# Attention probabilities turned in 32x32 blocks by VectorE, and their product with the values as four 32-row products side by side

## The chip, the cores and the metric

The kernel is one program on one core of a Trainium2 chip. The time is the device time of an execution in microseconds (us). All arithmetic is float32. TensorE (PE) multiplies a stationary operand (up to 128 rows by 128 columns, loaded by a weight load, PEld) with a moving one of up to 512 columns and writes to PSUM, which has eight banks of 512 float32 in each of 128 partitions. VectorE (DVE), ScalarE (ACT) and GpSimd (POOL) work elementwise; SyncE (SP) issues the DMAs.

## The reference, cut to what matters

The program is one encoder layer on two sequences, 1024 and 256 tokens, width 1024, with a recurrent branch, an attention branch, a merge and a feed-forward part. The change touches the attention branch only:

```python
# 8 query heads of 128, 2 key/value heads, head g of a group of 4 shares one key/value head
q = _apply_rope(_rmsnorm(q, q_norm), cos, sin)
k = _apply_rope(_rmsnorm(k, k_norm), cos, sin)
s = jnp.einsum('bqhgd,bkhd->bhgqk', qi, k).astype(jnp.float32) * scale   # scale = 128 ** -0.5
p = jax.nn.softmax(s, axis=-1).astype(v.dtype)
o = jnp.einsum('bhgqk,bkhd->bqhgd', p, v)
```

Each sequence attends within itself, without a mask.

## The kernel before

The layer is a row of stages (encoder_layer, L2028): attention_stage, then scaled_stage, gate_stage, state_stage, merge_stage and tail_stage, each in a Stage whose end is a barrier of all engines. Tokens of both sequences lie side by side, T = 1280 columns: 1024 of the first, 256 of the second.

attention_stage has two parts. The first projects ten heads (two for keys, eight for queries), normalises them and turns them by the position tables; the results lie in qk, head dimension on partitions. Then value_rows (L260) computes the values of ten blocks of 128 tokens and ACT copies them to vt, tokens on partitions. This part is not changed but for where its buffers lie.

The second part works on tiles of 128 queries. For a tile of the first sequence the keys are 1024, for one of the second 256; there are 64 tiles of the first kind and 16 of the second. The steps of a tile t, with c = t % 2 naming the buffer:

- scores(t), PE, L273: one or two products of 512 columns into PSUM banks 2c and 2c+1, queries on partitions, keys along the columns.
- maxima(t), DVE, L412: the maximum of each query over its keys, and that times the negative scale.
- exponents(t), ACT, L354: the exponential of all scores from PSUM to p[c], with the sums of the rows (an instruction of its own that reads the accumulator).
- normalise(t), DVE, L421: the reciprocal of the sum, and p times it.
- transposes(t), PE, L284: p turned in 128x128 blocks, through the identity, into banks 4 and 5.
- transposed(t), one half on ACT (L363) and one on DVE (L430): PSUM to pT, keys on partitions, queries along the columns.
- values(g, ks), PE, L293: for a group g of four tiles (512 queries of one head), or two for the second sequence, eight (two) products of 128 keys each, accumulated in bank 6 + g % 2, which gives the output with the head dimension on partitions.
- output(g), DVE, L439, and the send of it to HBM by SP, L221.

The order is written out by hand: PE does transposes(t), scores(t+2) and a quarter (half) of the value products of the group before, in turn. DVE does transposed(t), normalise(t+1), maxima(t+2) and, after a group's last tile, output(g-1). ACT does transposed(t) and exponents(t+2). Every engine works through its list in order, so an instruction that waits holds up all behind it. Semaphores (s_ready, exp_done, p_done, t_ready, o_ready and so on) carry the order between engines.

Other stages have products that use only part of the 128 rows of the array: in low_piece (L613 on) two of 64 rows, on partitions 0 to 63 and 64 to 127, for banks 6 and 7; in scores of state_stage (L1204 on) pairs of 64 rows and 192 columns for two banks; at L1272 and L1292 products of 32 rows, 32 stationary columns and 32 moving columns, at four different places of the array; at L636 products of 64 rows with 32 stationary columns. A float32 product is two MATMUL instructions (two passes) in the trace, a transpose is one.

Of the kernel before, what the change touches and what calls it, by code (L numbers as in the profile page):

```python
# [131 lines left out]
def attention_stage(nc, hbm, xT, cst, glob, w, ahead):  # L132

    with Stage(nc, "at") as st:
        NH = QH + KVH
        HEADS = (*range(QH, NH), *range(QH))
        cos, sin = st.sb("cos", 128, T), st.sb("sin", 128, T)
        qk = st.sb("qk", 128, NH, T)
        vt = st.sb("vt", 128, T // 128, KVH * HD)
        sq, rt, zr = st.sb("sq", 128, T), st.sb("rt", 128, T), st.sb("zr", 128, T)  # L140
        zq = [st.sb(f"zq{i}", 128, T) for i in range(2)]
# [11 lines left out]
        s_ready, mx_done, nm_done, exp_done, ri_done, p_done, t_ready, t_dve, t_act, o_ready, o_done = st.sems(  # L153
            "s_ready mx_done nm_done exp_done ri_done p_done t_ready t_dve t_act o_ready o_done")
        o_sent = st.sems("o_sent0 o_sent1")
        ones, ident = cst[:, C_ONES:C_ONES + 128], cst[:, C_ID:C_ID + 128]

        GROUPS = [(h, 512 * i, 0, SEQ_S, 4) for h in range(QH) for i in range(2)] + [(h, SEQ_S, SEQ_S, SEQ_P, 2) for h in range(QH)]
        TILES = [(g, i) for g, group in enumerate(GROUPS) for i in range(group[4])]
        FIRST = [sum(x[4] for x in GROUPS[:g]) for g in range(len(GROUPS))]  # L160
        NT = len(TILES)

# [3 lines left out]
        def keys_of(t):  # L166
            return GROUPS[TILES[t][0]][3]

# [4 lines left out]
        def columns(g):  # L173

            return 128 * GROUPS[g][4]

        def halves(t):

            return keys_of(t) // 256

        def values_after(t):

            g, i = TILES[t]
            if g == 0:
                return ()
            kt = GROUPS[g - 1][3] // 128
            n = GROUPS[g][4]
            return range(kt * i // n, kt * (i + 1) // n)
# [4 lines left out]
        def _(sp):  # L193
# [24 lines left out]
            sp.wait_ge(v_ready, T // 128)  # L218
            for c in range(2):
                sp.dma_start(w[:, c, :], hbm["w_in"][B_LOW + c]).then_inc(ahead[c], 16)  # L220
            for g in range(len(GROUPS)):  # L221
                h, t0, _, _, n = GROUPS[g]
                sp.wait_ge(o_done, g + 1)
                sp.dma_start(hbm["o_att"][:, h, t0:t0 + 128 * n], ot[g % 2][:, 0:128 * n]).then_inc(o_sent[g % 2], 16)
            for i in range(2):
                sp.wait_ge(o_sent[i], 16 * len(GROUPS[i::2]))

        @block.tensor
        def _(pe):
# [43 lines left out]
            def scores(t):  # L273
                g, i = TILES[t]
                h, t0, k0, nk, _ = GROUPS[g]
                if t >= 2:
                    pe.wait_ge(exp_done, t - 1)
                for b in range(0, nk, 512):
                    n = min(512, nk)
                    last = pe.matmul(ps[:, 2 * (t % 2) + b // 512, 0:n], qk[:, h, t0 + 128 * i:t0 + 128 * i + 128],  # L280
                                     qk[:, QH + h // (QH // KVH), k0 + b:k0 + b + n], start=True, stop=True)
                last.then_inc(s_ready, 1)

            def transposes(t):  # L284
                pe.wait_ge(p_done, t + 1)
                after(pe, t_dve, t)
                after(pe, t_act, t)
                n = halves(t)
                for k in range(2 * n):
                    last = pe.transpose(ps[:, 4 + k // n, 128 * (k % n):128 * (k % n) + 128], p[t % 2][:, 128 * k:128 * k + 128], ident)  # L290
                last.then_inc(t_ready, 1)

            def values(g, ks):  # L293
                h, _, k0, nk, _ = GROUPS[g]
                kv, n = h // (QH // KVH), columns(g)
                end = FIRST[g] + GROUPS[g][4]
                for k in ks:
                    if k == 0:
                        pe.wait_ge(t_dve, end)
                        pe.wait_ge(t_act, end)  # L300
                        if g >= 2:
                            pe.wait_ge(o_done, g - 1)
                    last = pe.matmul(ps[:, 6 + g % 2, 0:n], vt[:, k0 // 128 + k, HD * kv:HD * kv + HD], pT[g % 2][:, k, 0:n],  # L303
                                     start=(k == 0), stop=(k == nk // 128 - 1))
                    if k == nk // 128 - 1:
                        last.then_inc(o_ready, 1)
# [14 lines left out]
            for t in range(NT):  # L321
                transposes(t)
                if t + 2 < NT:
                    scores(t + 2)
                if TILES[t][0]:
                    values(TILES[t][0] - 1, values_after(t))
            values(len(GROUPS) - 1, range(GROUPS[-1][3] // 128))

        @block.scalar
        def _(act):  # L330
# [32 lines left out]
            def transposed(t):  # L363
                g, i = TILES[t]
                n = halves(t)
                act.wait_ge(t_ready, t + 1)
                if g >= 2 and i == 0:
                    act.wait_ge(o_ready, g - 1)
# [1792 lines left out]
```

## Time and profile before

| | us |
|---|---|
| median of three runs | 3450.26 |
| lowest, highest | 3448.57, 3451.94 |
| the profiled execution | 3442.2 |
| its span | 3440.3 |
| attention scores to last output, in it | 310.1 |

The span runs from the first to the last instruction of the profiled execution. In the trace, at_, ra_, rc_ ahead of a tensor's name is the stage (attention, scaled, state), and tensors from L280 on are those of the second part of attention_stage. A matmul's form names rows and columns of the stationary operand, then partitions and columns of the result. Matmul durations include the way through the array, so one lasts longer than the distance to the next; a run of them is read from start to start. "Idle before" is time in which the engine did nothing ahead of that group, with who ended it.

### The profile page before, as it was taken

How to read it: one execution, taken by the hardware profiler on the slowest of the kernel's cores; microseconds unless marked ns; L12 is line 12 of the kernel's file. 1: busy time of each engine (PE TensorE's matmuls, PEld its weight loads, DVE VectorE, ACT ScalarE, POOL GpSimd, SP SyncE). 2: the span in 40 equal slices, each digit the busy share in tenths (PEclk: the TensorE clock that was granted, in tenths of full speed). 3: DMA queues.
4: the chain of work that ended last, by engine and by line, in shares of the span. 5: the costliest groups of instructions: out<-in, count | busy, mean ns of one | idle time of the engine just before them, and what ended most of it. 6: DMA issues, size and time to landing. Idle time of an engine off the chain costs nothing. (4 is left out here: it accounts for less than half of the span.)

```text
span 3440.3 us, 57213 instructions
## 1 busy us (share of the span) xinstructions
PE 3266.6 (95%) x24648; PEld 2068.7 (60%) x24648; DVE 1830.0 (53%) x3086; ACT 986.6 (29%) x1570; POOL 2.5 (0%) x13
## 2 busy tenths in 40 slices
PE   9999998999999899978888999998999999999997
PEld 4565554555544455567777654566666666666665
DVE  1437773667766479145555432156554545645545
ACT  2334442334333223333333453001321121131121
POOL 0000000000000000000000000000000000000000
PEclk9999999999999999999999999999999999999998
DMA  3210001334543524255443223211121211222211
GB/s 134 69 42 13 16 16 41 118 118 134 177 137 111 185 71 162 103 187 176 146 149 117 85 86 131 105 37 61 46 71 61 82 60 61 74 75 80 78 62 61
DMA packets 200297, 321.76 MB, mean 94 GB/s; under 512 B 50800, under 2 KB 156272, under 8 KB 194928
## 3 DMA queue, kind: packets, MB, share of 16 engines
q1 hardware_dynamic: 200048, 318.12, 27.0%
q8 instruction: 196, 3.21, 0.4%
q14 instruction: 53, 0.43, 0.0%
HBM read 216.50 MB, written 95.03 MB: 91 GB/s over the span
## 5 line engine op out<-in xcount | busy, mean ns | idle before, releaser
L608 PE MATMUL ra_ps<-xT,ring 128*128 128x512 f32 (+1 forms) x1152 | 431.9, 528 | 0.0
L1730 PE MATMUL tl_ps<-merged,pool 128*128 128x320 f32 x1440 | 407.9, 436 | 6.4 <-PEq L108 3.9
L1730 PEld LDWEIGHTS tl_ps<-merged,pool 128*128 128x128 f32 x1440 | 274.9, 191 | 123.8 <-issue 11.9
L608 PEld LDWEIGHTS ra_ps<-xT,ring 128*128 128x128 f32 x1152 | 215.1, 190 | 200.4 <-issue 190.7
L1923 DVE TENSOR_TENSOR oR<-tl_ps,oR 128x320 f32<-128x320 f32 x416 | 202.2, 490 | 151.5 <-PE tl_ps L1730 149.4
L1046 PE MATMUL rg_ps<-xT,ring 128*128 128x512 f32 (+1 forms) x720 | 267.1, 526 | 11.9 <-PEq L108 11.9
L1730 PE MATMUL tl_ps<-tl_Th,pool 128*128 128x320 f32 x720 | 205.2, 436 | 6.1 <-issue 6.1
L1046 PEld LDWEIGHTS rg_ps<-xT,ring 128*128 128x128 f32 x720 | 135.1, 192 | 123.7 <-issue 118.2
L1811 ACT ACTIVATE ring<-tl_ps 128x320 f32<-128x320 f32 x96 | 42.0, 437 | 528.1 <-PE tl_ps L1730 528.1
L1730 PE MATMUL tl_ps<-xT,pool 128*128 128x320 f32 x640 | 182.7, 432 | 0.0
L1929 DVE TENSOR_TENSOR merged<-tl_ps,ring 128x320 f32<-128x320 f32 x96 | 47.2, 492 | 253.1 <-PE tl_ps L1730 135.0
L1730 PEld LDWEIGHTS tl_ps<-tl_Th,pool 128*128 128x128 f32 x720 | 138.2, 192 | 64.5 <-issue 8.3
L1730 PE MATMUL tl_ps<-merged,tl_sums 128*128 128x320 f32 x544 | 163.7, 440 | 12.8 <-DVE oR L1923 7.9
L1216 PE MATMUL rc_ps<-pool 64*128 64x192 f32 x1280 | 151.3, 367 | 12.1 <-POOL pool L1358 6.9
L254 PE MATMUL at_ps<-xT,ring 128*128 128x512 f32 (+1 forms) x432 | 159.1, 521 | 0.0
L1730 PEld LDWEIGHTS tl_ps<-xT,pool 128*128 128x128 f32 x640 | 121.6, 190 | 50.7
L1508 PE MATMUL mg_ps<-xT,ring 128*128 128x512 f32 (+1 forms) x384 | 143.4, 527 | 1.9 <-PEq L108 1.9
L1508 PE MATMUL mg_ps<-oR,ring 128*128 128x512 f32 (+1 forms) x384 | 139.4, 526 | 2.9 <-DVE oR L1561 2.9
L1730 PEld LDWEIGHTS tl_ps<-merged,tl_sums 128*128 128x128 f32 x544 | 103.4, 193 | 62.4 <-issue 23.0
L280 PE MATMUL at_ps<-at_qk 128*128 128x512 f32 (+1 forms) x288 | 130.0, 570 | 0.5 <-ACT at_vt L350 0.5
L360 ACT ACTIVATE at_p<-at_ps,at_nm 128x1024 f32<-128x1024 f32 (+1 forms) x80 | 79.0, 987 | 177.2 <-DVE at_nm L419 177.2
L303 PE MATMUL at_ps<-at_pT,at_vt 128*128 128x512 f32 (+1 forms) x288 | 129.4, 569 | 0.0
(241 smaller groups left out, 4747.9 us busy)
## 6 DMA issues: line engine op xcount, KB each, us to landing
pool<-ub SPq DMA_DIRECT2D x80, 640.0 KB, 5.3
ub<-ra_ub SPq DMA_DIRECT2D x32, 1280.0 KB, 5.4
pool<-in_w_ff SPq DMA_DIRECT2D x32, 1024.0 KB, 4.7
pool<-in_w_ff SPq DMA_DIRECT2D x64, 512.0 KB, 3.2
ring<-in_w_in SPq DMA_DIRECT2D x39, 512.0 KB, 3.4
xT<-in_xT SPq DMA_DIRECT2D x16, 640.0 KB, 8.1
ub<-ra_v SPq DMA_DIRECT2D x16, 640.0 KB, 6.5
mg_gate<-gates SPq DMA_DIRECT2D x16, 640.0 KB, 3.9
```

What stands on the lines that cost most here:

```text
L254: last = pe.matmul(ps[:, z_bank(i) + j, 0:n], w[:, i % 3, 128 * k:128 * k + 128], xT[:, k, t0:t0 + n], start=(k == 0), stop=(k == KT - 1))
L280: last = pe.matmul(ps[:, 2 * (t % 2) + b // 512, 0:n], qk[:, h, t0 + 128 * i:t0 + 128 * i + 128], qk[:, QH + h // (QH // KVH), k0 + b:k0 + ...
L303: last = pe.matmul(ps[:, 6 + g % 2, 0:n], vt[:, k0 // 128 + k, HD * kv:HD * kv + HD], pT[g % 2][:, k, 0:n], start=(k == 0), stop=(k == nk ...
L360: act.activation(p[c][:, 0:n], scores_of(t), ACT.Exp, bias=nm[:, c:c + 1], scale=ATT_SCALE, accum_out=rs[:, c:c + 1]).then_inc(exp_done, 1)
L608: last = pe.matmul(ps[:, bank + j, 0:n], w[c][:, 128 * i:128 * i + 128], xT[:, i, t0:t0 + n], start=(i == 0), stop=(i == KT - 1))
L1046: last = pe.matmul(ps[:, 3 * (b % 2) + j, 0:n], w[b % 3][:, 128 * i:128 * i + 128], xT[:, i, t0:t0 + n], start=(i == 0), stop=(i == KT - 1))
L1216: last = pe.matmul(ps[:, 4 + 2 * (q % 2) + h, 192 * j:192 * j + 192], x[rows, 2 * q + j, CH:3 * CH], x[rows, 2 * q + j, 3 * CH:6 * CH], st ...
L1508: last = pe.matmul(ps[:, 3 * (i % 2) + j, 0:n], w[i % 2][:, 128 * k:128 * k + 128], src[:, k, t0:t0 + n], start=(k == 0), stop=(k == KT - 1))
L1730: last = pe.matmul(bank(n, b), lhs(k), rhs(k), start=(fresh and k == 0), stop=(k == d - 1), skip_group_check=True)
L1811: act.activation(cp[n % 2][:, c, :], bank(n, b), ACT.Copy).then_inc(done, 1)
L1923: dve.tensor_tensor(y, bank(n, b), y, ALU.add).then_inc(done, 1)
L1929: dve.tensor_tensor(hidden(n, i, j), bank(n, b), cp[n % 2][:, c, :], ALU.add).then_inc(done, 1)
```

## The change

The 128x128 turns on PE and the copies of them out of PSUM are gone. Instead DVE turns each 32x32 block of p within its 32 partitions (turn), so that partition 32i + k of pT holds key 32j + k for the queries 32i to 32i + 31 of each tile. Quarter i of the partitions thus has its own queries and the keys of every block j. The product with the values (values) is, for each block of 32 keys, four products of 32 rows: quarter i of pT, 256 columns (32 queries of each of 8 tiles), with the 32 values of the block, into bank 4 + i. For this the values of a block must lie on each of the four quarters: they are written to HBM (vrow), and read back four times in rows of 128 numbers (spread) into v4, for the first key/value head ahead of the first group, for the second piece by piece as the last head of the first is done, for the second sequence likewise.

The scaling by the reciprocal goes from DVE to ACT (normalise), from SBUF to SBUF. A group is now one head's eight tiles (and for the second sequence two groups of eight tiles, four heads each): ten groups in place of 24. The value products of a group come in seven parts beside the next group's tiles 1 to 7. Its output, four banks of 256 columns, is copied by DVE (two banks) and ACT (two), and the next group's first products wait for these copies. The buffers of the projection part lie inside the two halves of pT, which are twice as large.

```diff
 with Stage(nc, "at") as st:
     NH = QH + KVH
     HEADS = (*range(QH, NH), *range(QH))
-    cos, sin = st.sb("cos", 128, T), st.sb("sin", 128, T)
     qk = st.sb("qk", 128, NH, T)
-    vt = st.sb("vt", 128, T // 128, KVH * HD)
...
     p = [st.sb(f"p{i}", 128, SEQ_S) for i in range(2)]
-    pT = [st.sb(f"pT{i}", 128, KT, 512) for i in range(2)]
-    ot = [st.sb(f"ot{i}", 128, 512) for i in range(2)]
+    turned = st.sb("turned", 128, 2 * 8 * SEQ_S)
+    v4 = st.sb("v4", 128, 32, HD)
+    ot = st.sb("ot", 128, SEQ_S)
+    cos, sin, sq, rt, zr, zq0, zq1 = (turned[:, T * i:T * i + T] for i in range(7))
+    zq = [zq0, zq1]
+    vt = turned[:, 7 * T:7 * T + 2 * T].rearrange("p (t c) -> p t c", c=KVH * HD)
+    pT = [turned[:, 8 * SEQ_S * c:8 * SEQ_S * c + 8 * SEQ_S].rearrange("p (j t q) -> p j t q", t=8, q=32) for c in range(2)]
...
+    s_ready, mx_done, nm_done, exp_done, ri_done, p_done, turn_done = st.sems(
+        "s_ready mx_done nm_done exp_done ri_done p_done turn_done")
+    v_stored, v4_ready, part_done, o_dve, o_act, o_sent = st.sems(
+        "v_stored v4_ready part_done o_dve o_act o_sent")
+    ones = cst[:, C_ONES:C_ONES + 128]
+    NG = QH + KVH
+    TILES = [(h, 128 * i, 0, SEQ_S) for h in range(QH) for i in range(8)]
+    TILES += [(h, SEQ_S + 128 * i, SEQ_S, SEQ_P) for h in range(QH) for i in range(2)]
     NT = len(TILES)
+    PARTS = 7
     def keys_of(t):
-        return GROUPS[TILES[t][0]][3]
+        return TILES[t][3]
     def scores_of(t):
         c = t % 2
         return ps[:, 2 * c:2 * c + 2, :].rearrange("p b n -> p (b n)")[:, 0:keys_of(t)]
-    def columns(g):
...
+    def blocks(g):
+        return 32 if g < QH else 8
+    def part(g, i):
+        n = blocks(g)
+        return range(n * i // PARTS, n * (i + 1) // PARTS)
+    def values_of(g, i, j):
+        at = j if g < QH else 8 * (g - QH) + j
+        return v4[32 * i:32 * i + 32, at, :]
+    def quarter(g, i):
+        return ot[:, :].rearrange("p (t i q) -> p i t q", i=4, q=32)[:, i], ps[:, 4 + i, 0:256].rearrange("p (t q) -> p t q", q=32)
     block = st.block()
...
-        sp.wait_ge(v_ready, T // 128)
+        def spread(dst, tokens, kv):
+            n = dst.stop - dst.start
+            for i in range(4):
+                sp.dma_start(v4[32 * i:32 * i + 32, dst, :],
+                             hbm["vrow"][tokens:tokens + 32 * n, HD * kv:HD * kv + HD].rearrange("(j k) d -> k j d", k=32)).then_inc(v4_ready, 16)
+        sp.wait_ge(v_done, T // 128)
         for c in range(2):
             sp.dma_start(w[:, c, :], hbm["w_in"][B_LOW + c]).then_inc(ahead[c], 16)
-        for g in range(len(GROUPS)):
...
+        sp.dma_start(hbm["vrow"].rearrange("(t p) c -> p t c", p=128), vt).then_inc(v_stored, 16)
+        sp.wait_ge(v_stored, 16)
+        spread(slice(0, 32), 0, 0)
+        for g in range(NG):
+            for i in range(PARTS):
+                if g in (QH // KVH - 1, QH - 1):
+                    js = part(g, i)
+                    if g == QH // KVH - 1:
+                        sp.wait_ge(part_done, PARTS * g + i + 1)
+                        spread(slice(js.start, js.stop), 32 * js.start, 1)
+                    elif i == 3:
+                        sp.wait_ge(part_done, PARTS * g + i + 1)
+                        for kv in range(KVH):
+                            spread(slice(8 * kv, 8 * kv + 8), SEQ_S, kv)
+            sp.wait_ge(o_dve, 2 * g + 2)
+            sp.wait_ge(o_act, 2 * g + 2)
+            if g < QH:
+                sp.dma_start(hbm["o_att"][:, g, 0:SEQ_S], ot[:, :]).then_inc(o_sent, 16)
+            else:
+                h = QH // KVH * (g - QH)
+                sp.dma_start(hbm["o_att"][:, h:h + 4, SEQ_S:T], ot[:, :].rearrange("p (h n) -> p h n", h=4)).then_inc(o_sent, 16)
+        sp.wait_ge(o_sent, 16 * NG)
     @block.tensor
     def _(pe):
...
             last.then_inc(v_ready, 1)
         def scores(t):
-            g, i = TILES[t]
-            h, t0, k0, nk, _ = GROUPS[g]
+            h, t0, k0, nk = TILES[t]
...
                 n = min(512, nk)
-                last = pe.matmul(ps[:, 2 * (t % 2) + b // 512, 0:n], qk[:, h, t0 + 128 * i:t0 + 128 * i + 128],
+                last = pe.matmul(ps[:, 2 * (t % 2) + b // 512, 0:n], qk[:, h, t0:t0 + 128],
                                  qk[:, QH + h // (QH // KVH), k0 + b:k0 + b + n], start=True, stop=True)
             last.then_inc(s_ready, 1)
-        def transposes(t):
...
+        def values(g, js):
+            for j in js:
+                if j == 0:
+                    pe.wait_ge(turn_done, 8 * g + 8)
+                    pe.wait_ge(v4_ready, 64 * (1 if g < QH // KVH else 1 + PARTS if g < QH else 3 + PARTS))
+                for i in range(4):
+                    if j == 0 and g:
+                        pe.wait_ge((o_dve, o_act)[i // 2], 2 * g - 1 + i % 2)
+                    last = pe.matmul(ps[:, 4 + i, 0:256], values_of(g, i, j), pT[g % 2][32 * i:32 * i + 32, j].rearrange("p t q -> p (t q)"),
+                                     start=(j == 0), stop=(j == blocks(g) - 1))
+            last.then_inc(part_done, 1)
         for i in range(NH):
             head(i)
...
         scores(0)
         scores(1)
         for t in range(NT):
-            transposes(t)
             if t + 2 < NT:
                 scores(t + 2)
-            if TILES[t][0]:
...
+            if t >= 8 and t % 8:
+                values(t // 8 - 1, part(t // 8 - 1, t % 8 - 1))
+        for i in range(PARTS):
+            values(NG - 1, part(NG - 1, i))
     @block.scalar
     def _(act):
...
             c, n = t % 2, keys_of(t)
             act.wait_ge(nm_done, t + 1)
             if t >= 2:
-                act.wait_ge(t_ready, t - 1)
-                act.wait_ge(ri_done, t - 1)
+                act.wait_ge(turn_done, t - 1)
             act.activation(p[c][:, 0:n], scores_of(t), ACT.Exp, bias=nm[:, c:c + 1], scale=ATT_SCALE,
                            accum_out=rs[:, c:c + 1]).then_inc(exp_done, 1)
-        def transposed(t):
...
+        def normalise(t):
+            c, n = t % 2, keys_of(t)
+            act.wait_ge(ri_done, t + 1)
+            act.activation(p[c][:, 0:n], p[c][:, 0:n], ACT.Copy, scale=ri[:, c:c + 1]).then_inc(p_done, 1)
+        def output(g):
+            act.wait_ge(part_done, PARTS * g + PARTS)
+            after(act, o_sent, 16 * g)
+            for i in range(2, 4):
+                dst, src = quarter(g, i)
+                act.activation(dst, src, ACT.Copy).then_inc(o_act, 1)
         exponents(0)
-        exponents(1)
         for t in range(NT):
-            transposed(t)
...
+            normalise(t)
+            if t + 1 < NT:
+                exponents(t + 1)
+            if t >= 16 and t % 8 == 0:
+                output(t // 8 - 2)
+        for g in range(NG - 2, NG):
+            output(g)
     @block.vector
     def _(dve):
...
             dve.wait_ge(s_ready, t + 1)
             dve.reduce_max(mx[:, c:c + 1], scores_of(t), AX.X).then_inc(mx_done, 1)
             dve.wait_ge(mx_done, t + 1)
-            if t >= 2:
-                dve.wait_ge(exp_done, t - 1)
             dve.tensor_scalar(nm[:, c:c + 1], mx[:, c:c + 1], -ATT_SCALE, None, ALU.mult).then_inc(nm_done, 1)
-        def normalise(t):
-            c, n = t % 2, keys_of(t)
+        def reciprocals(t):
+            c = t % 2
             dve.wait_ge(exp_done, t + 1)
-            if t >= 2:
-                dve.wait_ge(p_done, t - 1)
             dve.reciprocal(ri[:, c:c + 1], rs[:, c:c + 1]).then_inc(ri_done, 1)
-            dve.wait_ge(ri_done, t + 1)
...
+        def turn(t):
+            g, i, n = t // 8, t % 8, keys_of(t)
+            dve.wait_ge(p_done, t + 1)
+            if t == 8:
+                dve.wait_ge(v_stored, 16)
             if g >= 2 and i == 0:
-                dve.wait_ge(o_ready, g - 1)
...
+                dve.wait_ge(part_done, PARTS * (g - 1))
+            dve.transpose(pT[g % 2][:, 0:n // 32, i, :], p[t % 2][:, 0:n].rearrange("p (j k) -> p j k", k=32)).then_inc(turn_done, 1)
         def output(g):
-            n = columns(g)
...
+            dve.wait_ge(part_done, PARTS * g + PARTS)
+            after(dve, o_sent, 16 * g)
+            for i in range(2):
+                dst, src = quarter(g, i)
+                dve.tensor_copy(dst, src).then_inc(o_dve, 1)
         maxima(0)
+        reciprocals(0)
         maxima(1)
-        normalise(0)
         for t in range(NT):
-            g, i = TILES[t]
-            transposed(t)
+            turn(t)
             if t + 1 < NT:
-                normalise(t + 1)
+                reciprocals(t + 1)
             if t + 2 < NT:
                 maxima(t + 2)
-            if g and i == GROUPS[g][4] - 1:
...
+            if t >= 16 and t % 8 == 0:
+                output(t // 8 - 2)
+        for g in range(NG - 2, NG):
+            output(g)
...
 def encoder_layer(nc, hbm):
-for name, shape in (("o_att", [128, KT, T]), ("gates", [2 * KT, 128, T]), ("gd", [128, T]), ("bon", [PAIRS, 128, T]),
+for name, shape in (("o_att", [128, KT, T]), ("vrow", [T, KVH * HD]), ("gates", [2 * KT, 128, T]), ("gd", [128, T]), ("bon", [PAIRS, 128, T]),
```

## Rows read from the trace of the kernel before

**Rows 1.** The page: busy time of each engine, share of the span, instructions.

```profile
PE 3266.6 (95%) x24648; PEld 2068.7 (60%) x24648; DVE 1830.0 (53%) x3086; ACT 986.6 (29%) x1570; POOL 2.5 (0%) x13
```

**Rows 2.** Windows: stretch, length, busy time of engines (instructions), granted clock, DMA share, GB/s.

```profile
239.86:549.95 310.09, 297.48 (x1120) 163.49 (x1120) 218.41 (x424) 123.36 (x240) 0.00 (x0) 1.00 0.06 21
261.80:520.00 258.20, 258.20 (x961) 140.98 (x960) 182.22 (x319) 104.13 (x185) 0.00 (x0) 1.00 0.04 16
1500.00:1925.00 425.00, 374.06 (x11780) 324.15 (x11778) 233.76 (x517) 152.43 (x335) 0.00 (x0) 0.96 0.45 144
```

**Rows 3.** Timeline of PE: start us, length us, engine, line, operation, count.

```profile
402.69 1.88 PE L280 MATMUL at_ps<-at_qk 128*128 128x512 f32 x4
404.41 1.88 PE L303 MATMUL at_ps<-at_pT,at_vt 128*128 128x512 f32 x4
406.12 1.04 PE L290 MATMUL at_ps<-cst,at_p 128*128 128x128 f32 x8
407.00 1.88 PE L280 MATMUL at_ps<-at_qk 128*128 128x512 f32 x4
```

**Rows 4.** The timeline around L620.

```profile
593.68 0.59 PE L608 MATMUL ra_ps<-xT,ring 128*128 128x512 f32 x1
...
594.20 1.13 PE L620 MATMUL ra_ps<-low,ra_lw 64*128 64x512 f32 x4
...
595.26 0.70 PE L608 MATMUL ra_ps<-xT,ring 128*128 128x512 f32 x1
```

**Rows 5.** The timeline of PE at three runs of small products.

```profile
665.93 1.89 PE L636 MATMUL ra_ps<-ra_ub 64*32 64x32 f32 x160
...
1493.69 0.45 PE L1272 MATMUL rc_ps<-rc_rb,rc_SC 32*32 32x32 f32 x32
...
1496.74 1.57 PE L1216 MATMUL rc_ps<-pool 64*128 64x192 f32 x16
```

**Rows 6.** Groups of DVE by form: shapes, count, busy us, mean ns, idle before.

```profile
L415 DVE TENSOR_REDUCE at_mx<-at_ps 128x1 f32<-128x1024 f32 x64 | 78.4, 1224 | 24.3 <-PE at_ps L280 24.2
L428 DVE TENSOR_SCALAR at_p<-at_p,at_ri 128x1024 f32<-128x1024 f32 x64 | 48.2, 753 | 2.3
L869 DVE TENSOR_TENSOR_SCAN ra_cw<-ra_resets,ra_cw 128x256 f32<-128x256 f32 x80 | 47.4, 667 | 0.0
...
L426 DVE RECIPROCAL at_ri<-at_rs 128x1 f32<-128x1 f32 x80 | 12.4, 155 | 5.2 <-ACT at_p L360 4.7
...
L415 DVE TENSOR_REDUCE at_mx<-at_ps 128x1 f32<-128x256 f32 x16 | 6.7, 418 | 0.0
...
L444 DVE COPY at_ot<-at_ps 128x256 f32<-128x256 f32 x8 | 3.4, 424 | 0.8 <-PE at_ps L303 0.7
```

**Rows 7.** Groups of ACT by form.

```profile
L339 ACT ACTIVATE at_rt<-at_rt 128x1280 f32<-128x1280 f32 x10 | 12.7, 1270 | 0.1
...
L350 ACT ACTIVATE at_vt<-at_ps 128x256 f32<-128x256 f32 x10 | 3.8, 383 | 27.2 <-PE at_ps L269 27.2
```

**Rows 8.** The timeline where the scores begin.

```profile
239.86 3.70 PE L280 MATMUL at_ps<-at_qk 128*128 128x512 f32 x8 [0.47 <-ACT at_vt L350]
...
241.88 1.23 DVE L415 TENSOR_REDUCE at_mx<-at_ps 128x1 f32<-128x1024 f32 x1 [14.27 <-PE at_ps L280]
...
243.14 0.15 DVE L419 TENSOR_SCALAR at_nm<-at_mx 128x1 f32<-128x1 f32 x1
243.33 1.11 ACT L360 ACTIVATE at_p<-at_ps,at_nm 128x1024 f32<-128x1024 f32 x1 [3.52 <-DVE at_nm L419]
...
244.34 0.19 ACT L360 ACTIVATION_READ_ACCUMULATOR at_p<-at_ps,at_nm 128x1 f32 x1
```

**Rows 9.** DMA issues: tensors, queue, count, KB each, median us to landing.

```profile
rc_nb<-nb SPq DMA_DIRECT2D x20, 256.0 KB, 4.2
...
o_att<-at_ot SPq DMA_DIRECT2D x16, 256.0 KB, 2.0
...
o_att<-at_ot SPq DMA_DIRECT2D x8, 128.0 KB, 1.7
```

More of the change, by code:

```diff
@@ L152, in attention_stage @@
         v_ready, v_done = st.sems("v_ready v_done")
[L153 to L160, printed above, removed]
+        s_ready, mx_done, nm_done, exp_done, ri_done, p_done, turn_done = st.sems(
[6 more added lines that the diff above has]
+        TILES += [(h, SEQ_S + 128 * i, SEQ_S, SEQ_P) for h in range(QH) for i in range(2)]
         NT = len(TILES)
+        PARTS = 7
         def z_bank(i):
@@ L279, in scores @@
                     n = min(512, nk)
-                    last = pe.matmul(ps[:, 2 * (t % 2) + b // 512, 0:n], qk[:, h, t0 + 128 * i:t0 + 128 * i + 128],
+                    last = pe.matmul(ps[:, 2 * (t % 2) + b // 512, 0:n], qk[:, h, t0:t0 + 128],
                                      qk[:, QH + h // (QH // KVH), k0 + b:k0 + b + n], start=True, stop=True)
                 last.then_inc(s_ready, 1)
-            def transposes(t):
[L285 to L306, printed above, removed]
+            def values(g, js):
[9 more added lines that the diff above has]
+                last.then_inc(part_done, 1)
             for i in range(NH):
@@ L321, in _ @@
             for t in range(NT):
-                transposes(t)
                 if t + 2 < NT:
                     scores(t + 2)
-                if TILES[t][0]:
-                    values(TILES[t][0] - 1, values_after(t))
-            values(len(GROUPS) - 1, range(GROUPS[-1][3] // 128))
+                if t >= 8 and t % 8:
+                    values(t // 8 - 1, part(t // 8 - 1, t % 8 - 1))
+            for i in range(PARTS):
+                values(NG - 1, part(NG - 1, i))
         @block.scalar
@@ L357, in exponents @@
                 if t >= 2:
-                    act.wait_ge(t_ready, t - 1)
-                    act.wait_ge(ri_done, t - 1)
+                    act.wait_ge(turn_done, t - 1)
                 act.activation(p[c][:, 0:n], scores_of(t), ACT.Exp, bias=nm[:, c:c + 1], scale=ATT_SCALE,
                                accum_out=rs[:, c:c + 1]).then_inc(exp_done, 1)
-            def transposed(t):
[L364 to L368, printed above, removed]
-                act.activation(pT[g % 2][:, n:2 * n, 128 * i:128 * i + 128],
-                               ps[:, 5, 0:128 * n].rearrange("p (k q) -> p k q", q=128), ACT.Copy).then_inc(t_act, 1)
+            def normalise(t):
[8 more added lines that the diff above has]
+                    act.activation(dst, src, ACT.Copy).then_inc(o_act, 1)
             exponents(0)
-            exponents(1)
             for t in range(NT):
-                transposed(t)
-                if t + 2 < NT:
-                    exponents(t + 2)
+                normalise(t)
[5 more added lines that the diff above has]
+                output(g)
         @block.vector
@@ L446, in _ @@
             maxima(0)
+            reciprocals(0)
             maxima(1)
-            normalise(0)
             for t in range(NT):
-                g, i = TILES[t]
-                transposed(t)
+                turn(t)
                 if t + 1 < NT:
-                    normalise(t + 1)
+                    reciprocals(t + 1)
                 if t + 2 < NT:
                     maxima(t + 2)
-                if g and i == GROUPS[g][4] - 1:
-                    output(g - 1)
-            output(len(GROUPS) - 1)
+                if t >= 16 and t % 8 == 0:
+                    output(t // 8 - 2)
```

27 lines of the change are left out of this document (removed).

## The prediction

> **What bounds the kernel now.** I read the page's busy shares first: TensorE (PE) is busy for 95% of the span [rows 1]. The change touches one stage, so its windows came next: from the first score product to the last landing of an output it lasts 310.1 us, and from the first value product until the long tiles end PE is busy for 258.20 of 258.20 us, at a granted clock of 1.00 [rows 2]. VectorE (DVE) has 182 us in that stretch, ScalarE (ACT) 104. So PE sets the time there. The timeline gives its period: one score product of a 128x1024 tile takes 1.72 us, the share of value products that goes with it 1.71, eight transposes 0.88; together 4.31 us a tile [rows 3], and 64 tiles of that are 276 us.
>
> **What leaves PE.** The transposes: 0.88 us for each of 64 long tiles (56 us) and a quarter of that for the 16 short ones.
>
> **The value product.** One head had 16 products of 512 columns, each in two passes of 0.43 us (1.71/4), 13.7 us in all. Now it has 32 key blocks x 4 row groups x 2 passes of 256 columns. If the four groups run beside each other, PE streams 32 x 2 x 0.2145 = 13.7 us, the same. If they run one after another it is 54.9. What bears on this: with two row groups (L620, 64 rows each, outputs in two banks) four passes of 512 columns lie within 1.06 us, from 594.20 to 595.26, against 1.72 one after another; L1216 does 16 passes of 192 columns in 1.57 us, where one after another they need 16 x 0.16 = 2.6 [rows 4, 5]. With four groups of 32 rows only narrow products exist: 32 of 32 columns in 0.45 us, of which 0.19 is the last one's pipeline, so 8 ns each where 32 columns alone need 27 [rows 5]; but their outputs lie on different partitions, and here all four write the same 128 partitions, in four banks. Weight loads double with the groups too, but those of different groups start together: the two groups' products could not be that close otherwise. Issue is no limit: 160 small products lie within 1.89 us [rows 5], I need 8 in 0.43. Bounds: 13.7 to 54.9 us a head; I take 13.7, since both rows with two groups show no loss in steady streaming.
>
> **Changing between 128-row and 32-row products.** The last 128-row pass ahead of L620 starts at 593.68 and streams 0.43 us, to 594.11; L608 starts again at 595.26, and its first product takes 0.70 where others take 0.59 [rows 4]. Of these 1.15 + 0.11 us the two groups' streaming is 0.86. The round trip costs 0.40 us. A head's values come in 7 parts between scores: 7 x 0.40 = 2.8 us. Before, nothing of this kind stood there.
>
> **DVE and ACT per tile.** Removed: DVE's scaling (0.75) and its copy from PSUM, ACT's copy. Added on DVE: a 32x32 block transpose of 128x1024, which no row shows. Nearest is the reduce over the same elements, 1.22 us (L415), or 1.05 ns an element. Cheapest row on as many elements is 0.75 (L428); dearest per element the scan, (667 - 155)/256 = 2.0 ns, which would make 2.2 us [rows 6]. I take 1.22. Added on ACT: the scaling SBUF to SBUF. From 1.27 us for 1280 elements and 0.38 for 256, 1024 cost 1.27 - 256 x 0.87 ns = 1.05 us [rows 7].
> The new cycle of these two engines, from one reciprocal to the next: reciprocal 0.15, max 1.26 to the start of the negation, 0.15 of it, 0.04 until the exponential, 1.01 + 0.19 for that and its sum, 0.04 to the reciprocal: 2.85 us [rows 6, 8]. ACT's scaling (1.05) hides beside the max, DVE's turn beside the exponential: DVE's own sum is 0.15 + 1.26 + 0.15 + 1.22 = 2.8. PE needs 1.72 + (13.7 + 2.8)/8 = 3.8 us. PE stays the bound with about 0.9 us of cover; if the turn took 2.2 us the cover would be gone.
>
> **The border between heads.** Four banks hold one head's output and are no longer double. The next head's first values wait for two 128x256 copies on each of DVE and ACT (0.42 and 0.38 each [rows 6, 7]). DVE reaches them only behind the maximum of tile t+2, which waits for a score product that PE finishes just before: 0.2 + 1.41 + 0.85 = 2.45 us after it, while PE covers 1.72 with the next score product. Stall 0.75 us, taken as 0.8 (the DVE transpose queued behind the copies has slack).
> One head then is 8 x 1.72 + 13.7 + 2.8 + 0.8 = 31.1 us, against 8 x 4.31 = 34.5.
>
> **The loads of the values.** SP now writes the values to HBM (1.3 MB), waits, and reads them back spread (2.1 MB in 512-byte rows). 256 KB landed in 2.0 us where 128 KB took 1.7, so another 128 KB costs 0.3: 26 of them and two latencies are 11 us; at 4.2 us for every 256 KB one after another, the other extreme, 55 [rows 9]. The first value product needs them 32 us after the first scores. Hidden at the value I take; 24 us late at the extreme. The reload for the second key/value head follows head 3's parts and lands about 3.5 us after the last one (four issues, 2 us); PE has two score products (3.4) and the stall above there: nothing added. Behind this wait SP has only output sends, which nobody waits for then.
>
> **Sum**, in us from the first score product at 239.86:
> - Until head 0's values start. First reciprocal at 244.5 [rows 8], 4.7; eight cycles of 2.85 without values, 22.8; the scores of tile 11 wait for the exponential of tile 9 and end at 32.1; change of mode: 32.3. (Before, values started after 21.9; this is what deeper pipelining costs.)
> - Seven heads x 31.1 = 217.7.
> - Head 7's values beside short tiles: 13.7 + 2.7 + 6 scores of 0.43 = 19.0.
> - Eight short tiles at DVE/ACT's pace, 0.15 + 0.42 + 0.16 + 0.04 + 0.38 + 0.19 + 0.04 = 1.4 each: 11.0.
> - Tail: copies of the second last group 0.9, the last one's values 3.6 (before only the last of 24 groups was left, under 1 us), its copies 0.95, 512 KB out 2.7: 8.1.
>
> Together 288.1, against 310.1: 22 us less. The profiled execution took 3442.2 (span 3440.3), so it would be 3420; the median of the runs is 8.1 above that execution, and in its terms the forecast is 3450.3 - 22 = **3428 us**. Nothing else in the kernel moves: the projection part only has its tiles in other places.
>
> **Rivals.**
> 1. *The four row groups don't all stream at once.* Place: the value products; what could limit them is four writes to one PSUM partition at a time, where the rows show two. If they go in pairs, a head's values take 27.5 instead of 13.7. That is 13.8 more for each of 8 long heads and 3.4 for each of two short groups: +117, of which the short tiles' slack covers some 1.5, so about 3544, slower than before. It decides early: at 1.2 times the streaming time the gain of 22 is gone (22/117 of a doubling). For: no row with four groups on the same partitions. Against: two groups lose nothing, and narrow 32-row products run more than three at once. The Trainium skill gives a figure that speaks against this change: TensorE: Matmul & The Clock Gate, Measured speedup vs the span model, has 3.07 times for four row tiles of 32 at 512 columns. By that the eight heads and two short groups would gain 4/3.07 - 1 = 30% on 117 us of streaming, 35 us, and the time would be about 3463; no run here has such a product.
> 2. *The block transpose runs at the scan's pace, 2.2 us.* DVE's cycle is 3.8 us a tile and 0.85 of copies a head: the start grows by 7.6 us, each head by 1.3, the short tiles by 3: +20, 3448, no change. Against: the reduce, the scaling and the copies lie at 1.05 ns an element or below [rows 6]. The Trainium skill (Vector Engine (DVE) Microarchitecture Reference, The reshape front-end and per-opcode configuration) says that a transpose is pipelined to one element per cycle and lane, which is against this rival too; no row of this trace shows it.
> 3. *The values come late* (the extreme above): up to +24, 3452; a fraction is likelier. For: four loads with 4096 small rows. Against: the queue is empty there.
> 4. *The clock.* With 32-row products, or with PE busy 60% in the first 25 us, the granted clock falls to 1.2 GHz. At half the clock for the values alone: +117 and more, 3545. Against: the stretch with thousands of 64- and 32-row products has 0.96 while PE is busy 88% of it [rows 2].
> 5. *The change's saving isn't on the path.* Against: PE has no idle time in rows 2; I give it nothing beyond rival 2.
>
> **How the numbers follow.** Forecast 0.67, its own range 3416 to 3440 (change of mode between 0.2 and 0.6 us: 11 us either way over 56 round trips; a border stall of 0 to 2 us). Rival 1 0.13, rival 2 0.07, rival 3 0.05, rival 4 0.03, the rest (something costs about the gain) 0.05. 0.2% is 7 us, about what can be told from no change. Faster takes the forecast and nearly half of rivals 2 and 3: 0.72; same the other part of these and half the rest: 0.10; slower rivals 1 and 4 and what remains: 0.18. The range goes from 3412 to 3465, which takes in rivals 2 and 3 and the milder forms of rival 1, and leaves the full ones out.
>
> **What would show it.** In the new profile: value products of 256 columns of four groups starting together, with a fresh four every 0.21 us (rival 1: 0.43); 0.1 to 0.2 us holes where scores and values meet; DVE transposes of 1.22 us; ACT copies of 1.05; PE waiting about 0.8 us for the output copies eight or nine times; a head every 31 us; first values at 32 us in; stage of 288 us. The forecast is wrong if the four groups need more than 0.25 us, if the turn takes over 2 us, or if PE waits for a load.

## The result

The changed kernel takes 3407.61 us (3403.2 to 3411.5, four runs) against 3451.1 in the same series: ratio 0.987, 95% interval 0.9856 to 0.9885. A second series gave 0.9862 (0.9845 to 0.9879). It is faster by 44 to 48 us where 22 were forecast, and 3407.6 lies below the range. The profiled execution took 3403.2 us, its span is 3401.3 instead of 3440.3.

The windows of the changed kernel, to the barrier that ends each stage, answer to [rows 2]: the attention stage from the first score product, the stretch from head 0's first value product to head 7's, and the scaled stage.

```profile
243.30:524.12 280.82, 264.86 (x2464) 157.13 (x2464) 193.70 (x340) 173.26 (x260) 0.00 (x0) 1.00 0.16 47
274.64:486.37 211.73, 209.66 (x2009) 125.92 (x2009) 149.98 (x238) 132.98 (x184) 0.00 (x0) 1.00 0.08 26
524.12:1134.54 610.42, 597.90 (x4192) 308.07 (x4192) 399.10 (x483) 208.71 (x262) 0.60 (x6) 0.99 0.41 133
```

From the first scores to the barrier the stage takes 280.8 us; the kernel before has 310.6 there (239.86 to 550.42), so 29.7 us are won. The whole gain of 39 us in these two executions has more parts, in stages whose code is the same: the scaled stage has 610.4 us instead of 619.2, the state stage 460.3 instead of 467.9. Against that, the scores start 3.4 us later and the merge and tail stages are 4.1 us longer.

PE's timeline answers to [rows 3]; a row of 32 value products is four blocks, each with four row groups and two passes, and a row of 40 is five blocks. PE's wait for the output copies at the border between two heads is in the row at 305.34.

```profile
379.78 2.12 PE L317 MATMUL at_ps<-at_turned,at_v 32*128 32x256 f32 x36
381.83 1.98 PE L305 MATMUL at_ps<-at_qk 128*128 128x512 f32 x4
383.75 2.01 PE L317 MATMUL at_ps<-at_turned,at_v 32*128 32x256 f32 x32
385.68 1.98 PE L305 MATMUL at_ps<-at_qk 128*128 128x512 f32 x4
387.60 2.44 PE L317 MATMUL at_ps<-at_turned,at_v 32*128 32x256 f32 x40
```

```profile
305.34 2.24 PE L317 MATMUL at_ps<-at_turned,at_v 32*128 32x256 f32 x32 [0.21 <-DVE at_ot L456]
```

A score product and the change of mode take 1.92 us (381.83 to 383.75), four blocks of values with theirs 1.93. Streaming of four blocks is 8 x 0.2145 = 1.72, so the round trip costs 0.20 + 0.21, the 0.40 forecast. Four groups on the same partitions stream in the time of one: eight blocks take 3.67 us in experiment 8 (479.62 to 483.29) where four take 1.93, so a block costs 0.435 us, and two passes of one group alone are 0.429. The gain over one after another is thus 3.9 to 4.0. (The Trainium skill, TensorE: Matmul & The Clock Gate, Measured speedup vs the span model, has 3.07 for four row tiles at 512 columns; this trace, at 256 columns and in a steady stream, shows more.)

The groups by form, and then two rows of waits (us in total, times, longest):

```profile
L317 PE MATMUL at_ps<-at_turned,at_v 32*128 32x256 f32 x2176 | 137.0, 386 | 4.0 <-DVE at_ot L456 4.0
...
L449 DVE STREAM_TRANSPOSE at_turned<-at_p 128x1024 f32<-128x1024 f32 x64 | 79.1, 1236 | 7.1 <-PE at_ps L317 6.4 <-ACT at_p L378 0.7
L433 DVE TENSOR_REDUCE at_mx<-at_ps 128x1 f32<-128x1024 f32 x64 | 78.0, 1219 | 61.6 <-PE at_ps L305 61.2
L378 ACT ACTIVATE at_p<-at_p,at_ri 128x1024 f32<-128x1024 f32 x64 | 73.5, 1148 | 19.6 <-DVE at_ri L440 19.6
```

```profile
PE at_ps L305 <- ACT at_p L372: 7.9, 10, 1.0
...
PE at_ps L317 <- DVE at_ot L456: 4.0, 9, 1.2
```

### The profile page after: what moved, and what is told of

Read it like the earlier page. It is cut to its first block and busy times, and to the rows that moved or that the text cites. A ratio compares the mean times of both kernels' runs of the same rounds, so it can differ in the third digit from the quotient of the medians.

```text
span 3401.3 us, 59585 instructions
## 1 busy us (share of the span) xinstructions
PE 3227.4 (95%) x25992; PEld 2055.7 (60%) x25992; DVE 1803.5 (53%) x3002; ACT 1035.7 (30%) x1590; POOL 2.5 (0%) x13
## 5 line engine op out<-in xcount | busy, mean ns | idle before, releaser
L620 PE MATMUL ra_ps<-xT,ring 128*128 128x512 f32 (+1 forms) x1152 | 429.8, 526 | 0.0
L620 PEld LDWEIGHTS ra_ps<-xT,ring 128*128 128x128 f32 x1152 | 214.3, 190 | 198.9 <-issue 189.3
L1228 PE MATMUL rc_ps<-pool 64*128 64x192 f32 x1280 | 142.5, 349 | 11.7 <-POOL pool L1370 6.9
L317 PE MATMUL at_ps<-at_turned,at_v 32*128 32x256 f32 x2176 | 137.0, 386 | 4.0 <-DVE at_ot L456 4.0
L317 PEld LDWEIGHTS at_ps<-at_turned,at_v 32*128 32x128 f32 x2176 | 108.3, 184 | 49.1 <-issue 43.4
```

The lines of the kernel that those rows point to most:

```text
L317: last = pe.matmul(ps[:, 4 + i, 0:256], values_of(g, i, j), pT[g % 2][32 * i:32 * i + 32, j].rearrange("p t q -> p (t q)"), start=(j == 0) ...
L620: last = pe.matmul(ps[:, bank + j, 0:n], w[c][:, 128 * i:128 * i + 128], xT[:, i, t0:t0 + n], start=(i == 0), stop=(i == KT - 1))
L1228: last = pe.matmul(ps[:, 4 + 2 * (q % 2) + h, 192 * j:192 * j + 192], x[rows, 2 * q + j, CH:3 * CH], x[rows, 2 * q + j, 3 * CH:6 * CH], st ...
```

## Experiments

All ratios are to the kernel before on the same chip.

**1. Was the rest chance?** Both kernels again, for a second profile.

> The kernel before, unchanged, for a second profile of it. Open: of the 39 us between the two profiled spans, 26.3 lie in the attention stage and 12.7 in stages whose code is the same (8.8 in the scaled stage, 7.6 in the state stage, 3 to 4 lost again in the merge and tail stages). Theory A (it is where the instruction blocks of PE happen to end): a second profile shows the same stage lengths within 1.5 us, with a hole of some 4 us in the same run of small products at L636. Theory B (chance of one execution): the scaled and state stages differ by 5 us or more from the first profile. Time 3451, ratio 1.000.

> The changed kernel, unchanged, for a second profile. Theory A (position of the instruction blocks): scaled stage 610 us and state stage 460 again within 1.5 us each. Theory B (chance): one of them is off by 5 us or more. Time 3407, ratio 0.987.

Measured: 1.0001 (0.999 to 1.0013) and 0.9862. The windows of the kernel before, second profile (attention stage from the first scores, scaled stage):

```profile
239.90:550.47 310.57, 297.49 (x1120) 163.49 (x1120) 218.46 (x424) 123.38 (x240) 0.00 (x0) 1.00 0.06 21
550.47:1172.25 621.78, 601.46 (x4192) 309.38 (x4192) 399.18 (x483) 208.92 (x262) 0.60 (x6) 0.99 0.40 130
```

The attention stage repeats to 0.01 us (the changed one: 280.83), the scaled stage to 2.6 us (619.2, 621.8; changed 610.4, 612.9). The state stage does not: 467.9 and 471.3 before, 460.3 and 471.5 changed. The scaled stage moves by more than the 1.5 us that theory A allowed and by less than the 5 of theory B, but the 9 us between the kernels stay, and the second profile has its pause of PE at the same products of L636 as the first. In the state stage it is theory B: 460.3 was one lucky execution, and the other twelve profiles of this document have 467.9 to 480.9 there.

**2. Shifting PE's program.** Nine products of one column, 36 instructions (each product is two weight loads and two matmuls), behind PE's last value product of the kernel before:

```diff
             values(len(GROUPS) - 1, range(GROUPS[-1][3] // 128))
+            for _ in range(9):
+                pe.matmul(ps[0:32, 0, 0:1], cst[0:32, 0:32], cst[0:32, 0:1], start=True, stop=True)
```

> The kernel before with nine products of one column at the end of PE's part of the attention stage, 36 instructions, which brings the rest of PE's program to the same place within its blocks of 256 instructions as in the changed kernel (35 further). They lie in PE's idle time there. Theory A (position): scaled stage 610 us instead of 619, state stage near 460 instead of 468, time 3438, ratio 0.996. Theory B (chance) and theory C (addresses in HBM): same as before, 3451, ratio 1.000.

Measured: 3442.7 us, 0.9966 (0.9954 to 0.9978), 12 us faster. PE's timeline at one run of 160 small products, first without the nine (second profile of the kernel before), then with them:

```profile
1078.94 1.53 PE L636 MATMUL ra_ps<-ra_ub 64*32 64x32 f32 x154
1085.04 0.33 PE L636 MATMUL ra_ps<-ra_ub 64*32 64x32 f32 x6 [4.57 <-issue]
1085.30 5.49 PE L608 MATMUL ra_ps<-xT,ring 128*128 128x512 f32 x6
```

```profile
1080.17 1.58 PE L638 MATMUL ra_ps<-ra_ub 64*32 64x32 f32 x160
1081.69 3.70 PE L610 MATMUL ra_ps<-xT,ring 128*128 128x512 f32 x8
```

Without, PE stops 4.57 us ahead of the last six of 160 products, and the trace shows nothing that it waits for ("issue"). Such a stop is called a hole here. In the first profile the same hole lies at 1078.8 to 1083.1, and after PE has stopped the granted clock falls (windows of the kernel before; 0.59 and 0.73 are mixtures of full clock and 1.2 GHz):

```profile
1075.00:1080.00 5.00, 3.80 (x160) 2.18 (x158) 4.96 (x8) 0.00 (x0) 0.00 (x0) 1.00 0.97 319
1080.00:1085.00 5.00, 1.90 (x8) 1.03 (x9) 3.68 (x7) 1.35 (x2) 0.00 (x0) 0.59 0.15 57
1085.00:1090.00 5.00, 5.00 (x10) 2.05 (x9) 0.00 (x0) 0.72 (x1) 0.00 (x0) 0.73 0.64 262
```

The idle time ahead of the small products' weight loads (us, times), over all 16 such runs, in the second profile of the kernel before and with the nine products:

```profile
  issue: 26.9, 20
```

```profile
  issue: 11.3, 16
```

And the scaled stage of the kernel with nine products:

```profile
555.03:1165.78 610.75, 598.17 (x4192) 308.07 (x4192) 399.17 (x483) 208.91 (x262) 0.60 (x6) 0.99 0.41 133
```

So 8.4 to 11.0 of the 12 us lie in the scaled stage; where the rest lies this one profile doesn't tell. The state stage did not do what was expected: 474.9 us, not 460. The attention stage is 2.5 us longer from its first scores (313.1), and 1.7 longer in experiment 4, which adds nothing to PE's program; why is open.

**3. Shifting the changed kernel back**, with 55 such products, 220 instructions (36 short of 256).

> The changed kernel with 55 products of one column, 220 instructions, at the end of PE's part of the attention stage, in its idle time: the rest of PE's program lies again where it lay before the change within its blocks of 256 instructions. Theory A (position of the blocks): scaled stage 619 to 622 us instead of 610 to 613, with a hole near the small products of L636; time up by 9 to 12, 3420, ratio 0.989. Theory B (chance): 3409, ratio 0.986.

Measured: 3423.3 us, 0.9913 (0.9899 to 0.9926). Attention and scaled stage, and the idle time at the small products:

```profile
240.05:520.88 280.83, 268.45 (x2574) 161.05 (x2574) 193.73 (x340) 173.28 (x260) 0.00 (x0) 1.00 0.16 47
520.88:1140.42 619.54, 600.15 (x4192) 309.64 (x4192) 399.09 (x483) 208.71 (x262) 0.60 (x6) 0.99 0.40 131
```

```profile
  issue: 23.2, 20
```

The hole is back, and the attention stage is untouched. So place alone is worth 12 us in one direction and 15 to 18 in the other (7 to 9 of them in the scaled stage). The page lets one see why there are blocks: the changed kernel has this many loads of instructions

```profile
q8 instruction: 207, 3.39, 0.4%
```

which is 16 KB each; PE has by far the most instructions, 52,000 products and weight loads and 1,000 semaphore waits, so each load holds about 256. A run of 160 products is 320 PE instructions in 1.6 us, more than one such load.

The traces also show the load that comes late. In the second profile of the kernel before, the stretch from 1082.75 to 1083.75, inside the hole, has

```profile
q8 instruction: 1, 0.02, 5.8%
```

and there is none from 1080.5 to 1082.75: the load starts at 1082.80 and ends at 1083.72, and PE goes on at 1085.04. With the nine products the load for the same instructions ended at 1078.21, ahead of the whole run. Numbering PE's instructions (weight loads, matmuls, semaphore waits and barriers) in order of time in each trace, the first one behind a hole leaves the remainder 193 when divided by 256, in all twelve holes of over 1 us at these small products (six profiles), and starts 1.2 to 1.5 us after the end of a load. Nowhere in the thirteen profiles does an instruction with that remainder start less than 1.17 us after the end of its load. So the hole is PE waiting for a load. What makes the load start so late is open. The DMA engines are busy for 0.97 of the window ahead of the hole (1075 to 1080), but with the nine products, where there is no hole, also for 0.91 (1077.5 to 1082.5).

The scaled stage follows the holes: 610.4 to 612.9 us in the seven profiles that have none at the small products, 619.2 to 621.8 in the six that have them.

**4. Other addresses.** The new HBM tensor declared in the kernel before, unused.

> The kernel before with the new HBM tensor declared behind the first one and never used, so that all later ones lie 1.3 MB further, as in the changed kernel. Theory C (addresses in HBM change how fast the transfers of the state stage are): state stage near 460, time about 3440, ratio 0.997. Theories A and B: 3451, ratio 1.000.

Measured: 1.0001 (0.999 to 1.0013); scaled stage 619.9, with the hole at the same products (4.52 us), and state stage 478.1, not 460. Theory C falls.

**5. Other places**, the changed kernel with 18 and 36 such products.

> The changed kernel with 18 products of one column (72 instructions) at the end of PE's part of the attention stage. Theory A (position of the instruction blocks): the scaled stage is either 610 to 613 us, or 619 to 622 with a hole near the small products of L636, and the time follows it: 3409 or 3420. Theory B: 3409. Attention stage 280.8 from the first scores in both.

> The same with 36 products (144 instructions). Theory A: as in the kernel with 18, but each place has its own holes: the runs of small products there are 640 instructions long or more, so few places have none that costs; 3409 or 3420. Theory B: 3409.

Measured: 0.9914 (0.9901 to 0.9926) and 0.9918 (0.9905 to 0.9932); scaled stage 619.9 and 621.5, attention 280.8 in both. With 18 the holes are three smaller ones, with 36 one of 4.31 us in the first such run. Counted from the kernel before and by what is left over after whole loads of 256, the places tried are 0 (its own, and that of experiment 3, one short), 36 (experiment 2; the change's own 2595 more leave 35), 107 and 179. One of the four is good: the change happens to have it.

**6. The row groups in pairs**: in a part, all blocks of quarters 0 and 1 first, then of 2 and 3.

```diff
-                for j in js:
...
-                    for i in range(4):
+                for quarters in ((0, 1), (2, 3)):
+                  for j in js:
+                    for i in quarters:
```

> The changed kernel with a part's value products in another order: first all blocks of row groups 0 and 1, then all of groups 2 and 3. The number of products is the same. Theory F (groups stream fully beside each other, and only if issued next to each other): a head's streaming goes from 13.7 to 27.4 us; stage longer by 8 x 13.7 + 2 x 3.4 less some slack at the short tiles, 115 us; time 3524, ratio 1.020: this is what my first rival would have cost. Theory G (the queue ahead of PE lets groups 2 and 3 start while 0 and 1 still stream): clearly less, under 60 us.

Measured: 3480.7 us, 1.0084 (1.0069 to 1.0099); stage 348.9, longer by 68 us: between F (115) and G (under 60). PE's timeline:

```profile
400.44 2.98 PE L318 MATMUL at_ps<-at_turned,at_v 32*128 32x256 f32 x32
403.34 1.98 PE L305 MATMUL at_ps<-at_qk 128*128 128x512 f32 x4
```

Four blocks take 2.90 us instead of 1.93: 0.97 more where one pair after the other would be 1.72 more. Instruction by instruction, the first product of groups 2 and 3 starts at 401.42, 1.0 us after the part's first and 0.64 us before the last of groups 0 and 1: later products of free groups start early, but not from the beginning. The full gain needs the four groups issued close together; with them in pairs like this the change would have lost.

**7. DVE's cover**: each block transpose twice.

> The changed kernel with each block transpose done twice, the second behind the first, 1.24 us more on DVE for each long tile. If DVE and ACT have a cycle of about 2.9 us a tile beside PE's 3.87, DVE's becomes 4.1 and takes over: the start grows by 8 x 1.2 = 10 us, a head from 30.95 to 33.7 (19 us for seven), the short tiles by 4: plus 33 us, time 3442, ratio 0.996. If there were more cover than that, less than 15 us.

Measured: 3432.2 us, 0.9943 (0.9927 to 0.996); stage 300.4, 19.6 more instead of 33. DVE's timeline over one tile:

```profile
333.00 1.24 DVE L450 STREAM_TRANSPOSE at_turned<-at_p 128x1024 f32<-128x1024 f32 x1
334.27 1.25 DVE L452 STREAM_TRANSPOSE at_turned<-at_p 128x1024 f32<-128x1024 f32 x1
335.44 0.12 DVE L441 RECIPROCAL at_ri<-at_rs 128x1 f32<-128x1 f32 x1
335.49 1.20 DVE L434 TENSOR_REDUCE at_mx<-at_ps 128x1 f32<-128x1024 f32 x1
336.72 0.15 DVE L436 TENSOR_SCALAR at_nm<-at_mx 128x1 f32<-128x1 f32 x1
336.79 1.23 DVE L450 STREAM_TRANSPOSE at_turned<-at_p 128x1024 f32<-128x1024 f32 x1
```

DVE's cycle is 3.79 us with two transposes, not the 4.1 expected: the five instructions add up to 3.96, but small ones start before the one ahead has ended (335.44 under 334.27 + 1.25). It stays just under PE's 3.87, so a head grew by only 0.65 us (31.6), which is PE's longer wait for the output copies (0.88 instead of 0.23). The start grew by 8.3 us; the rest lies in the last two long heads, the short tiles and the tail. With one transpose, DVE and ACT set the pace only in the start, where the changed kernel's reciprocals come 2.75 us apart (256.24, 258.99; forecast 2.85).

**8. Fewer changes of mode**: four parts of eight blocks, beside every second tile.

```diff
-        PARTS = 7
+        PARTS = 4
...
-                if t >= 8 and t % 8:
-                    values(t // 8 - 1, part(t // 8 - 1, t % 8 - 1))
+                if t >= 8 and t % 2:
+                    values(t // 8 - 1, part(t // 8 - 1, t % 8 // 2))
```

> The changed kernel with a head's value products in four parts of 8 blocks, beside every second tile, instead of seven. Theory D (each change between 128-row and 32-row products costs PE 0.4 us there and back, and PE is the bound): three round trips fewer a head, 8 x 3 x 0.4 = 9.6 us, time 3400, ratio 0.9835. Theory E (the scores' two buffers can't bridge 3.4 us of values, PE waits for exponentials in between): stage no shorter, 3409 or more.

Measured: 3410.7 us, 0.9876 (0.9861 to 0.9891), no faster than the change; stage

```profile
240.19:519.58 279.39, 257.76 (x2464) 165.36 (x2464) 191.56 (x340) 173.97 (x260) 0.00 (x0) 0.98 0.16 47
```

Theory D holds for the long heads: five of them take 29.6 to 29.9 us from values to values instead of 30.95, mostly 29.72, which is 3 x 0.41 less. Theory E's time came, but not its reason: PE waits for exponentials 7.9 us in ten times, exactly as in the changed kernel. What takes the gain back is something else that the edit moved. SP reads the short sequence's values back (elif i == 3 in the diff) after a head 7 part that is the fourth of seven in the change, but the last of four here. Its loads and PE at that place:

```profile
479.62 3.74 PE L317 MATMUL at_ps<-at_turned,at_v 32*128 32x256 f32 x64
483.29 1.13 PE L305 MATMUL at_ps<-at_qk 128*128 128x256 f32 x4
...
492.74 1.13 PE L305 MATMUL at_ps<-at_qk 128*128 128x256 f32 x4
492.87 3.77 SPq L225 DMA_DIRECT2D at_v<-vrow  x8
...
499.51 2.09 PE L317 MATMUL at_ps<-at_turned,at_v 32*128 32x256 f32 x16 [5.64 <-DMA at_v<-vrow]
```

PE waits 5.64 us for them, and head 7 takes 24.85 us instead of 21.15; without that wait it would be 19 to 20 (an estimate: 24.85 - 5.64 = 19.2, and up to 0.7 for the output copies). The granted clock is 1.00 until 480 and falls once PE stands still there; what follows takes 20.1 us instead of 16.6, at a clock of 0.76:

```profile
499.51:519.58 20.07, 14.17 (x136) 10.89 (x136) 6.20 (x21) 5.49 (x16) 0.00 (x0) 0.76 0.16 57
```

**9. Four parts where theory D held**: heads 0 to 6 in four parts, the rest in seven. This also puts the short sequence's values back behind the fourth of seven parts.

> The changed kernel with heads 0 to 6 in four parts beside every second tile and the rest in seven parts as in the change. With four parts everywhere a head took 29.7 us instead of 30.95, but head 7 beside the short tiles 3.7 more and the short tiles 4 more. If both halves of that add up: stage from first scores to its end 280.8 - 7 x 1.23 = 272 us, time 3400, ratio 0.9837. If head 6's longer parts already starve the first short tiles: 275 and 3403.

Measured: 3404.4 us, 0.9849 (0.9831 to 0.9867); stage

```profile
242.77:514.98 272.21, 256.03 (x2464) 161.24 (x2464) 191.65 (x340) 174.01 (x260) 0.00 (x0) 1.00 0.17 49
```

272.2 us, as forecast, and PE waits for no load of values. The 3.7 and 4 us that the expectation gives to four parts beside the short tiles held the late load of experiment 8 and the lower clock behind it. Against the change's 0.9862 (0.9845 to 0.9879) the times don't separate, since the rest of the kernel varies by more, but the stage is shorter by 8.6 us, 7 x 1.23, in a place where five profiles of the change and its shifted forms agree to 0.02. Four parts for head 7 too, with its load issued earlier, was not run, so nothing shows that the short tiles need seven.

## Why the prediction was wrong

The direction was right, and so was the mechanism inside the attention stage; the size was half. The likely 3416 to 3440 and the range both missed. The stage alone, 29.7 us less, would have given 3450.3 - 29.7 = 3421, inside both: what took the time out of the range happened elsewhere.

The step that failed is "Nothing else in the kernel moves: the projection part only has its tiles in other places". PE's program before the scaled stage grew by 2595 instructions, and with that every later instruction lies elsewhere in its load of 256. This removes the holes at the small products of the scaled stage: 12 us of the gain by experiment 2, where the scaled stage has 610.8 us. With the program shifted back (experiment 3) the ratio is 0.9913, 30 us, just what the attention stage shows. These two make 42; measured were 44.9 (interval 40 to 50) and 47.6 (42 to 54). That the shift went the good way was luck: one place of four had no holes. What may be left is not settled; the state stage's 460 to 481 us over the profiles shows how much one execution can hide.

The terms of the sum, in us:

| term | forecast | profile after |
|---|---|---|
| until head 0's values | 32.3 | 31.3 |
| seven heads | 217.7 | 211.7 |
| head 7 | 19.0 | 21.2 |
| short tiles and tail | 19.1 | 16.6 |
| sum | 288.1 | 280.8 |

- The heads. Six took 30.7 to 30.95, forecast 31.1: streaming 13.7 and round trips 0.40 came true, the stall was shorter (below). The seventh took 26.3. I had put the short tiles' cheaper scores wholly into head 7, but scores run two tiles ahead, so three of them, 3 x 1.29 = 3.9 us, fall into head 6's stretch. The largest miss inside the stage is this one of bookkeeping.
- Short tiles and tail, 2.5 us less: I had charged the short tiles and the last group's values one after the other; probably they overlap more than that, but it was not tried apart. Head 7 took 2.2 more, so together the two are 0.3 off.
- The block transpose costs 1.24 us, taken 1.22 from the reduce; the scan's 2.2 of rival 2 was never near. (The 1.3 us a head of that rival don't follow from its own cycle: 8 x 3.8 + 0.85 is 31.25, 0.15 over the 31.1. Experiment 7, with 1.24 us more a tile, cost 0.65 a head.) ACT's scaling costs 1.15, taken 1.05: hidden either way.
- The border: PE waited for the copies nine times, 4.0 us in all: 0.21 to 0.23 at the six borders behind the long heads 0 to 5, then 0.71 twice and 1.24, where 0.8 was taken for each; the loads of the values came in time (rival 3 out), the clock is 1.00 in the stage (rival 4 out), and the four groups stream fully (rival 1 out).

## What to carry to other kernels

Where operands are split over the partitions anyway, four 32-row products issued next to each other into four banks cost what one 128-row product costs, and turning 32x32 blocks on DVE frees PE of transposes. The price is 0.4 us for each change between the two kinds of product and back, so make them in few long stretches; but see what else is counted in parts: with four parts a load of values came 5.6 us late.

Any change in the number of PE's instructions moves all later ones within their 16 KB loads, and here dense runs of tiny products won or lost 12 to 18 us by that. Before crediting a change, shift the old kernel's program to the same place, and compare stage by stage.

## What the runs showed of the hardware

- PE's instructions come in 16 KB loads of 256. Within 320 densely issued ones PE stood still for up to 4.6 us until 1.2 to 1.5 us after the end of a load; where the program lies in its loads decides whether that happens. Once PE had stopped the granted clock fell (0.59 and 0.73 in two windows of 5 us, that is, part of the time 1.2 GHz). 36 tiny instructions far ahead removed both. Twelve such holes at the small products of the scaled stage were looked at; the state stage has stops that end in the same way in all thirteen profiles, 32 to 44 of them with 48 to 64 us of idle PE, and no run tried to remove these.
- Four row groups of 32 writing the same 128 partitions in four banks: 0.435 us for a block of four against 0.429 for one group. In pairs one after the other four blocks took 2.90 us instead of 1.93, changes of mode included: 1.5 times, not 2, since later products of free groups start early.
- A 32x32 block transpose of 128x1024 float32 takes DVE 1.24 us, 128x256 0.44.
